# Reciprocal square roots of all norms: from logarithm and exponential on ScalarE to a power on GpSimd, in a two-layer MLA / GLA / MoE trunk

## The reference

```python
def rms_norm(x, g):
    xf = x.astype(jnp.float32)
    y = xf * lax.rsqrt(jnp.mean(xf * xf, axis=-1, keepdims=True) + EPS)
    return (y * g.astype(jnp.float32)).astype(x.dtype)
...
    for i in range(DEPTH):
        hn = rms_norm(h, norm_mix[i])
        h = h + (mla_mixer(hn, ...) if i % 2 == 0 else gla_mixer(hn, ...))
        h = h + hier_moe(rms_norm(h, norm_ffn[i]), ...)
```

## Time and profile before

| | us |
|---|---|
| median of 3 runs | 864.19 |
| lowest and highest run | 862.3, 866.5 |
| span of the profiled execution, first to last instruction | 862.8 |
| PE busy | 689.1 (80%) |
| PE weight loads busy | 387.4 (45%) |
| DVE busy | 248.8 (29%) |
| ACT busy | 210.6 (24%) |
| POOL busy | 41.9 (5%) |

### The profile page before, as it was taken

How to read it: one execution, slowest core, us unless ns; L and a number is a source line. 1 busy time by engine, 2 the same in 40 slices (tenths; PEclk the granted TensorE clock), 3 DMA queues, 4 the chain that set the end, 5 groups by cost and what they waited for, 6 DMA issues and landing times.

```text
span 862.8 us, 11600 instructions
## 1 busy us (share of the span) xinstructions
PE 689.1 (80%) x4878; PEld 387.4 (45%) x4878; DVE 248.8 (29%) x525; ACT 210.6 (24%) x382; POOL 41.9 (5%) x42
## 2 busy tenths in 40 slices
PE   3989599987888697887759999769688876686684
PEld 2634466455443442553338544354454432342341
DVE  3034676124322132132141202421422220221121
ACT  4343555351111111111132211243311111111110
POOL 3013100000000000000030001200000000000000
PEclk9999799998999988999989999889889988988897
DMA  8910180341999999999990514405539999999992
GB/s 294 334 14 1 62 329 2 137 182 72 382 410 413 416 413 412 415 416 410 415 376 1 194 30 166 194 1 194 196 114 414 416 410 415 415 413 412 415 415 103
DMA packets 56703, 233.41 MB, mean 271 GB/s; under 512 B 9473, under 2 KB 9537, under 8 KB 48097
## 3 DMA queue, kind: packets, MB, share of 16 engines
q1 hardware_dynamic: 56672, 232.98, 68.3%
HBM read 231.92 MB, written 1.05 MB: 270 GB/s over the span
## 4 chain that ended last, share of the span: by engine, by line
PE 51%; DMA 37%; DVE 5%; ACT 3%; issue 2%; SPq 1%; POOL 1%; POOLq 0%; DVEq 0%; ACTq 0%
DMA ring<-in_moe_w_down 36%; PE ps L816 10%; PE ps L596 6%; PE ps L866 6%; PE ps L857 4%; PE ps L671 3%; PE ps L803 2%; PE ps L633 2%; PE ps L784 2%; PE ps L825 2%; PE ps L621 1%; DMA ring<-in_mla_w_in 1%; PE ps L580 1%; PE ps L612 1%; PE ps L723 1%
## 5 line engine op out<-in xcount | busy, mean ns | idle before, releaser
L816 PE MATMUL ps<-ring,arena 128*32 128x512 f32 x512 | 84.7, 821 | 47.2 <-DMA ring<-in_moe_w_down 45.6
L803 PE MATMUL ps<-ring,arena 128*32 128x256 f32 x1536 | 88.4, 385 | 7.9 <-DMA ring<-in_moe_w_up 7.9
L784 PE MATMUL ps<-arena,xn 128*128 128x128 f32 x640 | 80.1, 287 | 12.6 <-DVE h L1435 10.8
L784 PEld LDWEIGHTS ps<-arena,xn 128*128 128x128 f32 x640 | 77.0, 201 | 25.0 <-DVE h L1435 23.1
L825 PE MATMUL ps<-arena 128*128 128x512 f32 (+1 forms) x160 | 73.4, 600 | 14.6 <-DVE arena L1430 14.6
L803 PEld LDWEIGHTS ps<-ring,arena 128*32 128x32 f32 x1536 | 49.1, 111 | 43.5 <-DMA ring<-in_moe_w_up 11.3
L816 PEld LDWEIGHTS ps<-ring,arena 128*32 128x32 f32 x512 | 19.3, 144 | 100.8 <-issue 52.1
L1435 DVE TENSOR_TENSOR h<-h,ps 128x512 f32<-128x512 f32 (+1 forms) x80 | 54.8, 684 | 32.5 <-PE ps L825 32.5
L866 PE MATMUL ps<-ring,hT 128*128 128x512 f32 x128 | 56.2, 595 | 0.0
L596 PE MATMUL ps<-ring,hT 128*128 128x512 f32 x128 | 55.7, 593 | 0.0
L825 PEld LDWEIGHTS ps<-arena 128*128 128x128 f32 (+1 forms) x160 | 25.4, 170 | 64.2 <-issue 64.2
(11 more groups left out here) (271 smaller groups left out, 785.8 us busy)
## 6 DMA issues: line engine op xcount, KB each, us to landing
ring<-in_moe_w_down SPq DMA_DIRECT2D x16, 4096.0 KB, 23.8
ring<-in_moe_w_gate SPq DMA_DIRECT2D x24, 2048.0 KB, 20.0
ring<-in_moe_w_up SPq DMA_DIRECT2D x24, 2048.0 KB, 23.5
arena<-in_moe_w_gate SPq DMA_DIRECT2D x8, 2048.0 KB, 28.2
arena<-in_moe_w_up SPq DMA_DIRECT2D x8, 2048.0 KB, 28.6
ring<-in_gla_w_in SPq DMA_DIRECT2D x3, 4096.0 KB, 25.2
ring<-in_mla_w_o SPq DMA_DIRECT2D x1, 4096.0 KB, 30.3
ring<-in_gla_w_o SPq DMA_DIRECT2D x1, 4096.0 KB, 14.6
```

Source lines behind the costliest of these rows:

```text
L784: mm = pe.matmul(ps[:, k // 4, (k % 4) * P:(k % 4 + 1) * P], xn[:, i, k, :], Sg[:, i, :], start=i == 0, stop=i == nt - 1)
L803: mm = pe.matmul(ps[32 * j:32 * j + 32, 2, m * FE:(m + 1) * FE], xe[:, k, 32 * j:32 * j + 32], w[:, m, j, kk * FE:(kk + 1) * FE], start=k ...
L816: mm = pe.matmul(ps[32 * j:32 * j + 32, 5 + b, :], hidT[:, k, 32 * j:32 * j + 32], moeD[:, j, k * D + b * 512:k * D + (b + 1) * 512], star ...
```

## The change

All logarithms and exponentials of the norms go from ScalarE. ScalarE only sums squares and raises the new semaphore `squares` after them. GpSimd waits for it, adds EPS with a multiply-add, raises the sum to the power -0.5 against a constant tile `mhalf` (48 columns of -0.5), and raises the semaphore that ScalarE raised before. In `norm(2)` and the router norms this lies on GpSimd between the work it had. For the keys, `head_scales` waits for the sums of squares alone. The query scales come after the keys of all tiles and are announced by a fourth count of `k_rstd`, for which VectorE waits ahead of L1298 and ScalarE ahead of its first exponential of the softmax. The Softplus and softmax exponentials stay on ScalarE.

```diff
-    fix = sb("fix", [P, 3])
-    eps_b, epsqk_b, one_b = (fix[:, i:i + 1] for i in range(3))
+    one_b = sb("one_b", [P, 1])[:, :]
+    mhalf = sb("mhalf", [P, 3 * HEADS])
...
+    FSQ = [0, 5, 8, 11]
...
+        def inverse_root(dst, v, eps, scale=1.0):
+
+            link(pool.tensor_scalar(v, v, scale, eps, ALU.mult, ALU.add))
+            return pool.tensor_tensor(dst, v, mhalf[:, 0:v.shape[1]], ALU.pow)
+
+        def norm_scales(n):
+
+            pool.wait_ge(squares, FSQ[n] + 2)
+            pool.wait_ge(m_squares, n // 2 + 1)
+            inverse_root(rstd[:, :], ssq[:, :], EPS).then_inc(rstd_ok, 1)
+
+        def route_scales(n):
+            for m, i in enumerate(ORDER[n]):
+                pool.wait_ge(squares, FSQ[n] + m + 1)
+                inverse_root(rstd[:, i:i + 1], ssq[:, i:i + 1], EPS).then_inc(rstd_ok, 1)
...
+        link(pool.memset(mhalf[:, :], -0.5))
...
+        norm_scales(0)
         meta_scaled(0)
+        for i in range(3):
+            pool.wait_ge(squares, 3 + i)
+            inverse_root(zrs[:, i, :], zst[:, i, :], EPS).then_inc(z_rstd, 1)
+
+        def head_scales(tiles):
+
+            pool.wait_ge(k_sums, tiles[-1] + 1)
+            for i in tiles:
+                n = HEADS if i < 2 else MH
+                inverse_root(krst[:, i, 0:n], kst[:, i, 0:n], EPS).then_inc(k_rstd, 1)
...
         queries_turned(0)
+        head_scales([0])
         keys_scaled(0)
         queries_turned(1)
+        head_scales([1, 2])
         keys_scaled(1)
         keys_scaled(2)
+        link(inverse_root(flat(scl[:, 0:2, :]), flat(qst[:, 0:2, :]), QK * EPS, float(QK)))
+        inverse_root(scl[:, 2, 0:MH], qst[:, 2, 0:MH], QK * EPS, float(QK)).then_inc(k_rstd, 1)
...
+        route_scales(1)
         pool.wait_ge(moe_done, 1)
         pool.memset(gv[:, 2, :], 0.0).then_inc(zeroed, 1)
         pool.memset(attM, 0.0).then_inc(zeroed, 1)
+        norm_scales(2)
         meta_scaled(2)
...
+        pool.wait_ge(squares, 11)
+        inverse_root(flat(gor), flat(gos), EPS).then_inc(g_orstd, 1)
+        route_scales(3)
...
         def scale_of(n, i):
 
-            link(square(n, i))
-            v = ssq[:, i:i + 1]
-            link(act.activation(v, v, ACT.Ln, bias=eps_b))
-            return act.activation(rstd[:, i:i + 1], v, ACT.Exp, scale=-0.5)
+            square(n, i).then_inc(squares, 1)
...
             for i in range(2):
-                ins = square(n, i)
-            link(ins)
-            act.wait_ge(m_squares, n // 2 + 1)
-            link(act.activation(ssq[:, :], ssq[:, :], ACT.Ln, bias=eps_b))
-            act.activation(rstd[:, :], ssq[:, :], ACT.Exp, scale=-0.5).then_inc(rstd_ok, 1)
+                square(n, i).then_inc(squares, 1)
...
-                link(act.activation(junk[rb_, QR:], ps[rb_, bb, 0:KVR], ACT.Square, scale=KVR ** -0.5,
-                                    accum_out=zst[rb_, i, 1:2]))
-                link(act.activation(zst[:, i, :], zst[:, i, :], ACT.Ln, bias=eps_b))
-                act.activation(zrs[:, i, :], zst[:, i, :], ACT.Exp, scale=-0.5).then_inc(z_rstd, 1)
+                act.activation(junk[rb_, QR:], ps[rb_, bb, 0:KVR], ACT.Square, scale=KVR ** -0.5,
+                               accum_out=zst[rb_, i, 1:2]).then_inc(squares, 1)
...
             copies(0)
-            scales([0], [])
             copies(1)
             copies(2)
             turned(0)
-            scales([1, 2], [0, 1, 2])
             turned(1)
             turned(2)
...
+            act.wait_ge(k_rstd, 4)
             act.wait_ge(mq_dif, 1)
...
             for i in ORDER[n]:
-                scale_of(n, i).then_inc(rstd_ok, 1)
+                scale_of(n, i)
                 act.wait_ge(rstd_ok, rstd_count(n, i))
...
-                    link(ins)
-            link(act.activation(flat(gos), flat(gos), ACT.Ln, bias=eps_b))
-            act.activation(flat(gor), flat(gos), ACT.Exp, scale=-0.5).then_inc(g_orstd, 1)
+                    if (t, g) != (1, GH - 1):
+                        link(ins)
+            ins.then_inc(squares, 1)
...
             dve.wait_ge(mq_s, 1)
+            dve.wait_ge(k_rstd, 4)
```

More of the change, by code:

```diff
@@ L250, in build @@
         act_link dve_link pool_link zeroed consts
-        m_squares rstd_ok xn_act xn_dve xn_pool xn_turned hT_ok
+        m_squares squares rstd_ok xn_act xn_dve xn_pool xn_turned hT_ok
         z_done z_rstd z_kr z_scaled c_turned cT_ok
@@ L262, in build @@
      act_link, dve_link, pool_link, zeroed, consts,
-     m_squares, rstd_ok, xn_act, xn_dve, xn_pool, xn_turned, hT_ok,
+     m_squares, squares, rstd_ok, xn_act, xn_dve, xn_pool, xn_turned, hT_ok,
      z_done, z_rstd, z_kr, z_scaled, c_turned, cT_ok,
@@ L510, in _ @@
         pool.memset(h[:, 2, :], 0.0).then_inc(zeroed, 1)
-        pool.memset(eps_b, EPS).then_inc(consts, 1)
-        pool.memset(epsqk_b, QK * EPS).then_inc(consts, 1)
         pool.memset(one_b, 1.0).then_inc(consts, 1)
+        link(pool.memset(mhalf[:, :], -0.5))
         pool.memset(vt[:, 2, :, :], 0.0).then_inc(zeroed, 1)
@@ L1151, in gla @@
                 ins.then_inc(g_yT_act, 1)
-        act.wait_ge(consts, 3)
+        act.wait_ge(consts, 1)
         norm(0)
```

## The result

The changed kernel takes 867.02 us (median of 20 runs, 864.7 to 868.46), the kernel before 863.08 us (median of 20, 859.28 to 867.09). The ratio is 1.0038 with a 95% interval of 1.0026 to 1.0051. The prediction was 857.7 us, a gain, with a range that ended at 864.

The account below looks back on a forecast made before the run. TensorE and DMA were taken to bound the kernel, norms counting only between TensorE work. Gains of 2.4 + 2.2 + 1.9 = 6.5 us off the 864.19 us median gave 857.7 us, range 854.0 to 864.0 (chance 0.70).

Parts of the forecast that it names:

- hidden by 1.4 us: Query scales after the keys: ready at 100.2 us, VectorE needs them at 101.6, so no cost.
- What bounds the kernel: TensorE and DMA carry 88% of the chain; norms count at three places: attention keys, layer 1 pre-norm, GLA output.
- r(N): Whole latency of multiply-add, power, link and two hops on GpSimd for N columns, estimated as 0.75 + 0.05 N us.
- The rival that the power costs per column: At every power: no gain at 0.19 us per column, slower above; chance 0.14 of over 0.5% slower.
- Key and query scales, -2.4 us: Ahead of attention: GpSimd starts on the key sums at once, key transposes start at 96.4 instead of 98.83 us.
- Contention with VectorE: At the key scaling on GpSimd: 2.09 us taken instead of 1.05; without contention the gain would be 3.4 us.
- Pre-norm of layer 1, -2.2: VectorE scales tile 0 about 1 us after the last sum instead of 3.23 us: 2.2 us gained.
- GLA output, -1.9: Norm of the GLA output: scaling starts 1.15 + 0.1 us after the sums instead of 3.16: 1.9 us gained.
- First norm, latents, routers: nothing: These norms are covered by weight transfer, VectorE's own work or TensorE, so no gain and no loss.
- Moved table loads: nothing: Loads may move to L1117 and L1073, where ScalarE idles 3.50 and 2.30 us, longer than 1.28: no cost.
- rival 2: Large fixed part, 1.5 to 2.2 us per pair, or dear first power: gain 0.8 to 3.6 us; shared chance 0.16.
- Rival 3: Chain doesn't move because something else comes up simultaneously, close only at the keys (3.4 us room); within a shared 0.16.

Follow-up runs that it names:

- e7: Changed kernel with each tile's keys scaled as soon as their own sums are there and query scales back on ScalarE: 860.13 us, 0.9964 of the kernel before.
- e3: Kernel before with only the key and query scales moved to GpSimd: 867.01 us, 1.0034 of the kernel before.
- e4: Changed kernel with most query powers moved ahead of the key sums and tile 1's keys not waiting for tile 2's: 862.69 us, 0.9987 of the kernel before.
- e11: Kernel before with the power at the pre-norm of layer 1 alone: 1.0008 of the kernel before.
- e10: Kernel of e9 with two idle GpSimd fills (0.95 us each) delaying the pre-norm of layer 1: 865.06 us, 1.0003 of the kernel before.
- e12: Kernel before with the power at the GLA output alone: 862.74 us, 0.9975 of the kernel before.
- e14: Kernel before with powers only at the first norm, the latents and the routers: 1.0010 of the kernel before.
- e2: Changed kernel with key and query scales back on ScalarE, all other norms as powers on GpSimd: 864.57 us, 1.0014 of the kernel before.
- e9: The kernel of e2 measured a second time, beside e10: 865.32 us, 1.0005 of the kernel before.

## Why the prediction was wrong, step by step

Two steps failed. The price of a power was taken as 0.05 us per column and is 0.157, so the query scales, "hidden by 1.4 us", held VectorE up by 2.99 us. And the gain at the pre-norm was counted as a gain at the end, where TensorE's clock took it back.

**What bounds the kernel.** Right in the places: the three that it named are the three that moved. Wrong in the sentence that a microsecond won ahead of the expert loop is won at the end. It was so at the keys (e7), but not at the pre-norm. Of the 1.9 us at the pre-norm, 1.8 were gone before the next projection.

**The price of a power.** This is the term that was mis-sized. Predicted: r(N) = 0.75 + 0.05 N. Measured: 0.2 for the multiply-add, 0.08 for the link and 0.40 + 0.157 N for the power, so 0.68 + 0.157 N, with the hops 0.1 more. The fixed part was right, the slope three times too small. For 3 columns it hardly matters (1.34 us with hops, for 1.0); for 8 it costs 0.8 us; for 32 it is 5.7 instead of 2.35. The rival that the power costs per column had the right mechanism. Its formula gives 12.9 - 67 x 0.157 = 2.4 us of gain for this slope, and 1.3 with the measured fixed part (0.68 for 0.5 in six pairs); by the start times it was 0.8 us (1.9 + 1.1 - 2.2). So the slope takes most of the forecast away but doesn't make the kernel slower by itself; the rest is the clock and what stays open below.

**Key and query scales, -2.4 us; measured +2.2.** Three parts. The powers of the keys alone took 2.91 + 1.01 us, where 1.55 + 0.95 stood for powers, multiply-adds, links and hops together. A multiply-add of 4 columns took 1.24 us, beside VectorE's key scaling. The key scaling itself escaped and took 1.05. So the transposes started 6.8 us after the key sums, for 7.2 before, and 4.7 were predicted. Then came the sentence "hidden by 1.4 us": the query scales needed 7.1 us instead of 3.3 behind the keys (99.49 to 106.60), and VectorE idled 2.99 us for them. This is the row (timeline of VectorE after), the counterpart of the L1298 row:

```profile
106.70 0.23 DVE L1311 TENSOR_REDUCE arena<-ps 128x4 f32<-128x64 f32 x1 [2.99 <-POOL arena L508]
```

e3 shows that this place alone costs 0.34%, and e4 that moving the queries' powers ahead takes it away. The prediction named the wrong-if condition itself, a 32-column power of over 4 us; its range, which ended at 864.0, made no room for it.

**Contention with VectorE.** It was there: the earlier trace rows showed 2.09 against 1.05 us, and the runs showed it on other instructions too (3.17 us in e4, 1.24 and 1.06 for 0.20 after and in e7). The two short ones ended within 0.1 us of VectorE's instruction (at 96.70 after and 95.10 in e7), as if they had waited for it. It goes the other way too: VectorE's key scaling of 256 columns took 1.26 us after, where GpSimd's had begun first, and 0.42 in e7, where VectorE's had. The Trainium skill (GPSIMD Engine Reference, Specifications) has the two engines share their way to SBUF, with contention when a VectorE instruction reads two operands from it or runs in a two-port mode. The short rows agree, since L1272 (L1284 after, L1296 in e7) is of the first kind. The 2.09 us of e7 lay beside L1317, which reads PSUM; whether that one is of the second kind no row shows.

**Pre-norm of layer 1, -2.2; measured -1.9, then +1.8.** The start time was right, the term in the sum was not: it left out that TensorE's clock may come back later behind the shorter idle time. e11 has no gain (1.0008), and e10 no loss when the gain is put back.

**GLA output, -1.9; measured -1.1.** r(8) was 1.95 us and the whole 2.07 us for 1.25. Some of it survives (e12), how much is open.

**First norm, latents, routers: nothing.** Right in the traces; in the times up to 2.5 us aren't excluded (e14). The first projection still waited for the weights (TensorE idle 2.42 us ahead of it instead of 0.25), and the other landmarks stay.

**Moved table loads: nothing.** Right. A load now stands in front of L1117 and L1073, in ScalarE's idle time, before its wait is over (1.00 us to spare at L1073, 2.21 at L1117). In front of L1073 (L1085 after):

```profile
623.61 1.28 ACT L1085 ACT_TABLE_LOAD   x1
625.89 0.21 ACT L1085 ACTIVATE arena<-arena 128x10 f32<-128x10 f32 x1 [1.00 <-DVE arena L1395]
```

**Sum.** The three terms add up as written. But the span of 862.8 us isn't that of an execution near the lowest time: spans are some 1.9 us shorter than the times (865.2 and 867.07 us after), so that execution took about 864.7 us (an estimate), near the median. The forecast for the median, 864.19 less 6.5, stays the same by it.

**The other rivals.** A dear first power (rival 2): no. (The gain of that rival was summed wrong: by the prediction's own terms it is 11.1 us less four times the price of a pair, so 5.1 to 2.3 us, and not 3.6 to 0.8.) The first took 0.86 us for 3 columns, the same shape later has a mean of 0.864. The 6 us that the Trainium skill (GPSIMD Engine Reference, Instruction dispatch) names for the first call of newly loaded code are not seen at the power; whether its code is of that kind no run shows. Rival 3 (something else comes up at the same time) had no chance of its own and called only the keys close; the clock is a form of it.

What stays open: the sum. By the start times e2 and e9 should lie 3.0 us below before. The clock behind the pre-norm takes 1.8 of them in most executions and the slower output projection 0.4 to 0.7, which leaves 0.5 to 0.8 us below before. Measured are 1.2 above (0.3 below to 2.7 above) for e2 and 0.4 above (1.0 below to 1.9 above) for e9. The first interval excludes what the terms add up to, the second only just holds it. So 1 to 2 us of the change's loss have no cause shown. The norms called hidden (theory C) could hold them, and e14 leaves room for that.

## What to carry to other kernels

Price a function on GpSimd by its columns. Here a power cost 0.157 us a column, so it beat the pair of table loads (3.1 us) up to some 15 columns in latency and lost beyond (an estimate from 0.78 + 0.157 us per column); put the narrow ones there, and start the wide ones where the engine idles. When a wait in front of TensorE gets shorter, look at the clock behind it: the same 16 products took 3.84 or 5.6 us, and that was as much as the wait had won. Before an engine's idle time is shortened, ask with a cheap experiment, a delay put in, whether the path feels it at all.

## What the hardware showed that was not expected

- GpSimd's power is linear in its columns over 1 to 32: 0.555, 0.710, 0.864, 1.010, 1.667, 2.906, 5.423 us for 1, 2, 3, 4, 8, 16, 32.
- A GpSimd instruction of 4 columns took 1.24 us instead of 0.20 while VectorE ran a long one with two SBUF operands; one of 512 columns took 2.09 and 3.17 instead of 1.05 beside VectorE's work.
- TensorE's clock did not come back in proportion to work done. After 8.7 us of idle time it was back 3.4 us after TensorE resumed, after 6.9 us only after 9 us; in e9, after 6.8 us, it was back after 3.2. The attention layer, unchanged from its first softmax step on, took 47.4 to 50.5 us in the profiles of kernels that run it alike. From 105 to 156 us the clock was never low in the shortest of them (e9) and for 9.6 us in the longest (e10).
- 56 and 50 idle transposes in two waits made the kernel before 0.36% faster (0.9941 to 0.9987), at a mean granted clock of 0.938 instead of 0.928.
